# Half-precision passes for the second half of a filter's transform, placed behind the first projections' second token halves

## The reference

```
hy, q, k, v, nq, nk, nv = split(modulate(rms_norm(x)) @ w_in)   # hy: 768 columns
filt = hyena_filter(...)        # sine network, times a decay: forward and backward taps, 256 channels
u = short_conv(hy)              # 3 taps along the tokens, 768 channels: v, x1, x2
v = v * x1
y = irfft(rfft(v, 2S) * rfft(filt, 2S))[:S]
out = x2 * (y + v * skip)
```

## Time and profile before

| | us |
|---|---|
| median of three timed runs | 1261.15 (1258.84 to 1262.37) |
| the profiled execution | 1259.79 |
| its span, first to last instruction | 1258.0 |
| PE busy | 1228.7 (98%) |
| DVE busy | 975.1 (78%) |
| ACT busy | 657.3 (52%) |
| POOL busy | 402.0 (32%) |
| granted TensorE clock, mean | 0.999 of full |

### The profile page before, as it was taken

How to read it: one execution, slowest core, us unless ns; L and a number is a source line. 1 busy time by engine, 2 the same in 40 slices (tenths; PEclk the granted TensorE clock), 3 DMA queues, 4 the chain that set the end, 5 groups by cost and what they waited for, 6 DMA issues and landing times. The chain is left out here.

```text
span 1258.0 us, 23349 instructions
## 1 busy us (share of the span) xinstructions
PE 1228.7 (98%) x8052; PEld 667.3 (53%) x8052; DVE 975.1 (78%) x1583; ACT 657.3 (52%) x1244; POOL 402.0 (32%) x381
## 2 busy tenths in 40 slices
PE   8999999999999999999999999999999999999997
PEld 1564656556675666664454455455545554444443
DVE  3879998676778999964379888888888885666587
ACT  2632234556779999963135644555455553412425
POOL 0100000114678999850031244455544430000001
PEclk9999999999999999999999999999999999999999
DMA  9728723235200130021300332322233307997953
GB/s 355 276 75 327 253 83 134 68 90 154 65 31 2 34 134 5 29 85 51 117 34 2 101 91 87 96 73 74 83 98 100 100 25 260 350 335 248 357 205 134
DMA packets 111030, 164.16 MB, mean 130 GB/s; under 512 B 8560, under 2 KB 70000, under 8 KB 109552
## 3 DMA queue, kind: packets, MB, share of 16 engines
q1 hardware_dynamic: 110960, 163.24, 37.8%
HBM read 138.57 MB, written 22.55 MB: 128 GB/s over the span
## 5 line engine op out<-in xcount | busy, mean ns | idle before, releaser
L1307 PE MATMUL PS<-arena 128*128 128x512 f16 (+9 forms) x7452 | 1187.2, 320 | 18.0 <-DMA arena<-in_w_mod 5.4
L1307 PEld LDWEIGHTS PS<-arena 128*128 128x128 f16 (+3 forms) x7452 | 616.5, 100 | 562.7 <-issue 37.9
L3094 DVE SCALAR_TENSOR_TENSOR arena<-arena 128x512 f16<-128x512 f32 x128 | 113.2, 890 | 29.8 <-ACT arena L2342 29.3
L2342 ACT ACTIVATE arena<-arena 128x512 f16<-128x512 f32 x120 | 75.3, 630 | 98.5 <-PE PS L1307 98.5
L2470 ACT ACTIVATE arena<-arena 128x512 f16<-128x512 f32 x77 | 48.1, 629 | 126.2 <-DVE arena L3314 75.1
L2986 DVE TENSOR_REDUCE arena<-PS 128x1 f32<-128x512 f32 (+1 forms) x160 | 106.5, 680 | 9.1 <-PE PS L1307 9.1
L2241 ACT ACTIVATE arena<-PS 128x512 f16<-128x512 f32 x140 | 88.3, 631 | 1.2 <-PE PS L1307 0.7
L1301 POOL TENSOR_TENSOR arena<-arena 128x1 f32<-128x1 f32 x8 | 4.8, 606 | 232.1 <-DVE arena L3468 232.1
L1157 POOL TENSOR_TENSOR arena<-arena 128x512 f16<-128x512 f32 x64 | 74.0, 1159 | 9.4 <-ACT arena L2244 8.1
L3151 DVE TENSOR_TENSOR arena<-PS,arena 128x256 f32<-128x256 f32 (+1 forms) x100 | 55.1, 552 | 24.8 <-PE PS L1307 24.5
L3010 DVE TENSOR_TENSOR arena<-PS,arena 128x512 f16<-128x512 f32 x96 | 65.4, 682 | 4.0 <-ACT PS L2244 3.9
(11 more groups left out here) (220 smaller groups left out, 1287.3 us busy)
## 6 DMA issues: line engine op xcount, KB each, us to landing
arena<-in_w_ffn_out SPq DMA_DIRECT2D x121, 256.0 KB, 5.0
arena<-in_w_mod SPq DMA_DIRECT2D x23, 1024.0 KB, 7.3
arena<-in_w_ffn_in SPq DMA_DIRECT2D x88, 256.0 KB, 3.0
left_operands<-arena SPq DMA_DIRECT2D x43, 256.0 KB, 3.0
arena<-in_w_in SPq DMA_DIRECT2D x9, 1024.0 KB, 5.5
arena<-left_operands SPq DMA_DIRECT2D x3, 2816.0 KB, 13.0
arena<-lay_bias SPq DMA_DIRECT2D x12, 512.0 KB, 3.9
arena<-in_x SPq DMA_DIRECT2D x2, 2048.0 KB, 13.5
```

The costliest lines, as they stand in the source:

```text
L1307: return pe.matmul(out, lhsT, rhs, start=start, stop=stop, skip_group_check=True)
L2342: act.activation(block_split(p, b)[:, 0], weight_block(p, b), ACT.Copy, scale=WS).then_inc(blk_hi, 1)
L3094: dve.scalar_tensor_tensor(dst[:, 1], src, WS, dst[:, 0], ALU.mult, ALU.subtract).then_inc(blk_lo, 1)
```

## The change

The second half of the filter's transform (kt = 1) is done in three f16 passes instead of f32. Its table comes as high and low halves (fwd2, scaled by 2^10; the same 1 MB), and the taps are split into halves too (filt16, neg16, scaled by 2^8): four copies on ACT and four subtractions on DVE, made after the last tokens have been split. The first half of the transform (kt = 0) stays in f32. The 24 products become 72. They stand behind the second token halves of ct 0 and 1 now, where they stood ahead of them. On ACT and DVE the work that needs the spectrum moves behind the convolution of ct 1, with the half of chunk 11 behind that of ct 0. Late product 1 comes behind the spectrum, late 2 and 3 behind it.

```
+            def filter_sums_16():
+                c = chunk_index("ff", 1)
+                arrived(pe, c)
+                w = raw16(c, NT * 2, 2, P)
+                even, odd = (0, 1), (2, 3, 6, 7)
+                high = (4, 5)
...
+                    pe.wait_ge(filt_lo, 1 + ready + 1)
+                    for bank, cols, parts in groups:
+                        for i, (nt, trig, src) in enumerate(parts):
+                            for part, other in ((0, 0), (0, 1), (1, 0)):
+                                ins = mm(PS[:, bank, 256 * cols:256 * cols + 256], w[:, 2 * nt + trig, part], src[:, other],
+                                         i == 0 and part + other == 0, i == len(parts) - 1 and part == 1)
+                ins.then_inc(spec_mm, 1)
...
-            arrived(pe, chunk_index("ff", 1))
+            pe.wait_ge(hT_rdy, 16)
+            for ct in range(2):
+                pe.wait_ge(hT_f, 19 + ct)
+                hyena(ct, (1,))
             pe.wait_ge(spec_rdy, 1)
-            for part in range(6):
-                filter_sums(1, part)
-            pe.wait_ge(hT_rdy, 16)
-            pe.wait_ge(hT_f, 20)
-            for ct in range(2):
-                hyena(ct, (1,))
+            filter_sums_16()
...
-            even_filter(1)
-            hi_of(chunk_index("hy", 1), spl(1, KD, 256))
+            for n, (dst, src, scale) in enumerate((
+                    (filt16[:, 0, 0], filt_a, FS), (filt16[:, 0, 1], filt_b, FS),
+                    (neg16[:, 0, 0], filt_a[:, 6:8], -FS), (neg16[:, 0, 1], filt_b[:, 2:4], -FS))):
+                act.activation(flat(dst), flat(src), ACT.Copy, scale=scale).then_inc(even_part, 1)
...
+                if ct == 0:
+                    act.wait_ge(spec_mm, 1)
+                    hi_of(chunk_index("hy", 1), spl(1, KD, 256))
                 if ct == 1:
+                    even_filter(1)
                     hi_of(chunk_index("hy", 2), spl(0, KD, 256))
...
             late(0)
-            filter_spectrum(1)
-            lo_of(chunk_index("hy", 1), spl(1, KD, 256))
+            for n, (dst, hi, src, scale) in enumerate((
...
+                dve.wait_ge(even_part, 3 + n + 1)
+                dve.scalar_tensor_tensor(flat(dst), flat(src), scale, flat(hi), ALU.mult, ALU.subtract).then_inc(filt_lo, 1)
...
+                if ct == 0:
+                    lo_of(chunk_index("hy", 1), spl(1, KD, 256))
                 if ct == 1:
+                    filter_spectrum(1)
+                    late(1)
                     lo_of(chunk_index("hy", 2), spl(0, KD, 256))
-                for n in ((1, 2), (3,), (4, 5), (6, 7), (), ())[ct]:
+                for n in ((), (2, 3), (4, 5), (6, 7), (), ())[ct]:
```

More of the change, by code:

```diff
@@ L36 @@
 CV, CG = 2.0 ** -3, 2.0 ** 2
+FS = 2.0 ** 8
 MAGIC = 1.5 * 2.0 ** 23
@@ L489, in build @@
         neg_a, neg_b = f32(44, 2, HYW), f32(46, 2, HYW)
+        filt16 = f16(Z + 59, 2, 2, NT, HYW)
+        neg16 = f16(Z + 75, 2, 2, 2, HYW)
         xs = f32(Z + 59, 10, D)
@@ L675, in build @@
         left_in["A22"], left_in["S3"] = near_in[1], x_in[1]
+        filt_lo = mcol_mm
         part_hi, part_lo = taps_mm, taps_rdy
@@ L882, in load @@
                         sp.wait_ge(split_lo, n_split(before))
-                sp.dma_start((raw16 if CHUNKS[c] in ("fwd", "inv") else raw)(c, *shape), src).then_inc(raw_in[chunk_slot(c)], 16)
+                sp.dma_start((raw16 if CHUNKS[c] in ("fwd", "inv") or c == chunk_index("ff", 1) else raw)(c, *shape), src).then_inc(raw_in[chunk_slot(c)], 16)
             sp.dma_start(cols[:, 0:N_COLS], lay["cols"]).then_inc(cols_in, 16)
@@ L910, in _ @@
                     load(c, w_in[:, :, 256 * n:256 * n + 256], (8, 256))
+                elif kind == "ff" and n == 0:
+                    load(c, cst["fwd"][n].rearrange("p a b k -> p (a b) k"), (16, P))
                 elif kind == "ff":
-                    load(c, cst["fwd"][n].rearrange("p a b k -> p (a b) k"), (16, P))
+                    load(c, cst["fwd2"][n].rearrange("p a b c k -> p (a b c) k"), (32, P))
                 elif kind == "fwd":
@@ L1364, in filter_sums @@
                         .then_inc(spec_mm, 1)
+            def filter_sums_16():
[4 more added lines that the diff above has]
+                high = (4, 5)
+                for ready, groups in enumerate((
+                        [(4, 0, [(nt, 0, filt16[:, :, 0, nt]) for nt in even]),
+                         (5, 0, [(nt, 0, filt16[:, :, 0, nt]) for nt in high]),
+                         (6, 0, [(nt, 0, filt16[:, :, 0, nt]) for nt in odd])],
+                        [(4, 1, [(nt, 1, filt16[:, :, 1, nt]) for nt in even]),
+                         (5, 1, [(nt, 1, filt16[:, :, 1, nt]) for nt in high]),
+                         (6, 1, [(nt, 1, filt16[:, :, 1, nt]) for nt in odd])],
+                        [(7, 0, [(nt, 1, filt16[:, :, 0, nt] if nt < 4 else neg16[:, :, 0, nt - 6]) for nt in odd])],
+                        [(7, 1, [(nt, 0, neg16[:, :, 1, nt - 2] if nt < 4 else filt16[:, :, 1, nt]) for nt in odd])])):
+                    pe.wait_ge(filt_lo, 1 + ready + 1)
[5 more added lines that the diff above has]
+                ins.then_inc(spec_mm, 1)
             def forward(kt):
@@ L2666, in filter_spectrum @@
             def filter_spectrum(kt):
-                a = CG / (1024 * TS * CV)
+                a = CG / (1024 * TS * CV) / (TS * FS if kt else 1)
                 f = [flat(F[:, kt, j]) for j in range(4)]
-                dve.wait_ge(even_part, 2 + kt + 1)
+                dve.wait_ge(even_part, 2 + 5 * kt + 1)
                 own.step(dve.scalar_tensor_tensor(fp, PS[:, 5], a, f0, ALU.mult, ALU.add))
@@ L2718, in _ @@
             late(0)
-            filter_spectrum(1)
-            lo_of(chunk_index("hy", 1), spl(1, KD, 256))
+            for n, (dst, hi, src, scale) in enumerate((
+                    (filt16[:, 1, 0], filt16[:, 0, 0], filt_a, FS), (filt16[:, 1, 1], filt16[:, 0, 1], filt_b, FS),
+                    (neg16[:, 1, 0], neg16[:, 0, 0], filt_a[:, 6:8], -FS), (neg16[:, 1, 1], neg16[:, 0, 1], filt_b[:, 2:4], -FS))):
+                dve.wait_ge(even_part, 3 + n + 1)
+                dve.scalar_tensor_tensor(flat(dst), flat(src), scale, flat(hi), ALU.mult, ALU.subtract).then_inc(filt_lo, 1)
             for ct in range(6):
@@ L2766, in residue_sums @@
                 (a, b, c, d), bank = half_sums, lambda n: PS[:, n].rearrange("p (a k) -> p a k", a=2)
-                dve.wait_ge(even_part, 4 + 2 * kt + 1)
+                dve.wait_ge(even_part, 8 + 2 * kt + 1)
                 own.step(dve.tensor_tensor(a, r0, bank(5), ALU.add))
                 own.step(dve.tensor_tensor(b, r0, bank(5), ALU.subtract))
-                dve.wait_ge(even_part, 4 + 2 * kt + 2)
+                dve.wait_ge(even_part, 8 + 2 * kt + 2)
                 own.step(dve.tensor_tensor(c, r1, bank(7), ALU.add))
```

2 lines of the change are left out of this document (1 added, 1 removed).

## The result

| | before | after |
|---|---|---|
| median of 20 timed runs each, side by side, us | 1259.07 | 1263.12 |
| all runs, us | 1257.47 to 1263.59 | 1261.15 to 1267.93 |
| ratio to before, with its 95% interval | | 1.0027 [1.002, 1.0034] |
| span of the profiled execution, us | 1258.0 | 1262.6 |
| PE / DVE / ACT busy, us | 1228.7 / 975.1 / 657.3 | 1230.1 / 980.9 / 660.8 |

A forecast was written before the change was run, and what follows sets the result against it. PE was taken as the bound, DVE close behind: minus 2.65 us for the products plus 5.25 us of new waits gave +2.6 us, so 1263.1 us from the mean of four runs, 1260.54; range 1258 to 1266.3 us.

The forecast's parts named there:

- PE is the bound, DVE close behind.: From 60 to 300 us PE waited only 3.3 us; DVE's lateness by 122 us reaches PE at 174.40 us.
- The products: 7.86 instead of 10.5 us, and the transform's end at 97.05 us.: Second filter transform on PE: 72 half-precision products replace 24 full-precision ones, saving 2.65 us, running from 89.2 to 97.05 us.
- The splits: no PE wait.: ScalarE's copies done by 85.1 us, DVE's subtractions by 89.25 us, covered by 10.4 us of moved projections; no PE wait.
- The chain through DVE.: After the later-freed slot, DVE waits for late weights; third convolution starts at 115.6 us, 3.0 us late, 2.6 remaining.
- the data stream was continuous, so its landing shifts by the same 7.75 us: Late product 2's weight, queued behind the filter table's slot, lands at 110.45 us instead of 102.7 us.
- rival 2: Late weights 2 and 3 land together at 112.95 us, late product 2 starts 2.5 us later; sum +5.1 us, chance 0.15.
- PE's two meetings.: PE waits 3.6 us for late product 7 near 130 us, then meets DVE again at 174.40 us.
- At 174.40 us it is behind by all of DVE's 2.6 us.: At the transposes of the query, key and value part, PE is late by DVE's remaining delay, 2.6 us.
- A shift at 174.40 us stays to the end.: After 174.40 us PE waits only 2.1 us near 298 us, behind engines that follow PE, so the delay persists.
- Rival 1: PE's saving from the products comes through: minus 2.65 us, 1257.9 us; chance 0.12.
- Rival 3: Queued transfers drain faster and DVE waits little or not at all; sum -1.5 to -0.2 us, chance 0.12.
- Rival 4: PE waits for a split near 89 us because a ScalarE copy starts late; with 2 us, 1265 us; chance 0.03.

The follow-up runs named there:

- Run 2: Kernel before, with only SP's order edited: third projection weight and rope tables issued ahead of late weight 1; 1260.67 us, ratio 0.9995 to before.
- run 10: Changed kernel with third weight and rope tables issued first, rope scaling in DVE's wait near 198 us, late columns behind v's first transposes; 1257.29 us, 0.9970 of before.
- run 11: Kernel before with three rearrangements (SP issue order, rope scaling in DVE's wait, columns behind transposes), transform in full precision at its old place; 1261.12 us, 0.9997 of before.
- run 4: Kernel before with the splits' four copies and four subtractions added, results unread, transform still f32 in its old place; 1262.56 us, ratio 1.0006 to before.
- run 6: Half-precision transform with its splits at the old place and in the old order, without the two projections as cover; 1265.95 us, ratio 1.0041 to before.
- Run 3: Changed kernel with 15 unused products keeping PE busy ahead of the second late group's columns; 1263.15 us, ratio 1.0018 to before.
- run 1: Changed kernel with the third projection weight and rope tables issued on SP ahead of late weight 1; 1258.60 us, ratio 0.9982 to before.
- run 5: Changed kernel's order with the transform's second half still in f32 and no splits, the move alone; 1267.89 us, ratio 1.0055 to before.
- run 7: Changed kernel with only the two rope tables issued later, behind the load of late product 5; 1262.57 us, ratio 1.0013 to before.
- run 9: Changed kernel with third weight and rope tables issued first, and rope scaling moved into DVE's wait near 198 us; 1259.50 us, ratio 0.9983 to before.
- run 8: Changed kernel with third weight and rope tables issued first, and rope scaling on DVE moved to about 225 us; 1261.80 us, ratio 1.0000 to before.

## Why the prediction was right, and where it was not

**PE is the bound, DVE close behind.** Right. Run 2 shows it from the other side: in before, DVE's third convolution 1.5 us earlier only made DVE wait for PE at the next one.

**The products: 7.86 instead of 10.5 us, and the transform's end at 97.05 us.** Right: ACT's copy behind it starts at 97.05 us, forecast 97.15. What they are worth in time is less clear: by run 10 against run 11, 3.8 us of medians, but 1.4 to 1.9 us at T.

**The splits: no PE wait.** Right, by the trace and by run 4; without the cover 6.66 us, by run 6. ACT took 4.74 us for the four copies and DVE 5.69 for the four subtractions, where I had 5.0 and 5.94.

**The chain through DVE.** The waits came where they were said to be: 1.74, 0.97, 2.20, 0.89 and 1.08 us, against 1.2, 0.8, 2.3, 1.0 and "just in time". The landings were forecast at 102.3, 105.3, 110.45 and 112.95 and came at 102.4, 105.4, 110.5 and 114.3. The last one is a miss of 1.35 us: of "the data stream was continuous, so its landing shifts by the same 7.75 us" only three of four held. The window from 110.5 to 114.3 us moved 1.54 MB, at 405 GB/s; late weight 3 is 1.05 MB of that at most. The rest, 0.49 MB at least, is of weights issued later: of late weight 4, issued at 105.17 us, 5.3 us behind it, and perhaps of the next, issued at 109.7 us. By the Trainium skill (DMA: Bandwidth & Descriptors, Queues, rings and completion order) descriptors of a ring are taken in ring order but completions need not follow it; the trace goes no further than that: the weights landed in the order of their issue, but a later one moved data before an earlier one had landed. I had weighed it for weights 2 and 3 (rival 2), not for a weight issued much later. With it the third convolution was 4.3 us late, not 3.0.

**PE's two meetings.** The wait for the late columns came at 3.36 us plus 1.46 us before the projection in front of them, 4.8 instead of 3.6. The forecast didn't name the meeting at that projection; with the third convolution at the forecast 115.6 us it would have come to some 0.1 us. The transposes of v started 3.0 us later than before. Here the forecast had PE 1 us behind; most of the difference is that 1.35 us landing and about 0.5 us of columns at the lower clock (above).

**The step that failed: "At 174.40 us it is behind by all of DVE's 2.6 us."** It was behind by 5.7. Between the transposes of v and T stand 2.75 us (0.76 + 1.99) in which PE did the same work at half the clock. The forecast had no term for that; a wait of 3.6 us stood in it at full price and no more. With the DVE chain alone, 4.3 less the regained 0.5 us, T would have come 3.8 us late; the clock made PE later than DVE, and DVE waited for PE's transposes instead (1.8 us in all between 123 and 200 us). Run 3 shows the term: with PE kept busy T is 2.0 to 2.1 us earlier, counted from the same start, and PE waits for DVE again.

**"A shift at 174.40 us stays to the end."** Not all of it. Up to the attention's last such transposes it does: from T to them PE takes 108.6 us before and 108.7 with the change. Then the wait of 2.1 us near 298 us is 0.56 here, with another of 0.25 behind it, and span less T is 1.1 us shorter (1082.5 against 1083.6). At T the late landing adds 1.2 us to the forecast of 2.6 and the clock another 1.9 beyond DVE's 3.8: 5.7 us, less the 1.1 given back is the span's 4.6. The timed runs put the change at 3.4 to 4.05. So a landing that was put too early and a clock that wasn't counted, with some given back, stand behind a time that came out as forecast.

**The rivals.** Rival 1 (the saving comes through) needs DVE not to be late; with SP's order changed it nearly is so, in run 1, and in run 10. Rival 2 (the two weights land together) fails by the trace: 110.5 and 114.3 us, 3.8 us apart. Rival 3 fails: the fourth megabyte landed 13.5 us after the first was issued (97.0 to 110.5), as before, and not 10. Rival 4 fails, as said. Two side sums of the forecast are slightly off, with no bearing on it: 4 MiB in about 10 us from 97.1 us land near 107.1 us, not 107.6, and 1.1 us sooner with 0.5 regained is -1.6 us, not -1.5.

**What stays open.** PE's wait near 300 us was 0.5 to 4.35 us long in the thirteen traces: 2.1 in before, 0.56 with the change, 4.35 in run 4, 1.9 in run 10. It doesn't follow T, and in some traces the clock falls behind it, as here in run 4:

```profile
300.12 2.05 PE L1311 MATMUL PS<-arena 128*128 128x384 f16 x21 [4.35 <-DVE arena L2978]
```

```profile
295.00:300.00 5.00, 0.78 (x4) 0.16 (x2) 0.49 (x2) 1.33 (x4) 1.25 (x1) 0.91 0.31 17
300.00:305.00 5.00, 4.88 (x31) 3.33 (x32) 2.31 (x8) 2.88 (x8) 1.16 (x1) 0.50 0.97 356
```

PE, DVE and ACT all stand nearly still there while little data moves (17 GB/s). No run was made to find its cause, and one trace of each kernel can't tell how often it is short. The length alone doesn't decide whether the clock falls: it fell after 1.99 us in run 5, and not after 2.07 us in before and in run 7. It is a likely part of the several us by which executions of one kernel differ: of the 79 timed runs of before beside the experiments, the 19 with a mean granted clock of 0.999 took 1260.2 us on average, the 6 with 0.996 took 1263.5 us. Where in these runs the clock fell isn't recorded. So the 1.1 us given back are read from one trace of each kernel, and whether the change or chance did it isn't shown; nor is it shown why the medians of runs 5, 9, 10 and 11 differ by other amounts than their T.

## What to carry to other kernels

Moving work that frees a buffer moves everything that stands behind that buffer's next load in the issuing queue, needed or not: before such a move, look which of the queued transfers need the slot at all, and issue the others first. A saving on the bounding engine is kept only if the engine next to it, here DVE, is early by as much at the next place where they meet. And price a new wait on PE with what may follow it: in this kernel 3.4 us of waiting cost PE another 2.75 us (and some 0.5 more in the columns) at the lower clock, of which some 2 us arrived at the attention.

## What the runs showed of the hardware

- The granted clock fell to 0.50 after PE waits of 3.36 us (the change), 3.35 (run 5), 2.89 (run 7) and 6.66 (run 6), but also after one of 0.45 us (run 8); it did not after 0.58 (run 1), 0.71 (run 9), 1.36 (run 3) and 1.46 us (the change, before its fifth projection). The length of one wait alone does not decide it. In the change, and in runs 5, 7 and 8, the work right behind the wait was sixteen products of one column; but runs 1 and 9 had these too, without a fall.
- Transfers of 1 MB that were issued 5.3 us and more behind another on the same queue took part of the data rate before the first had landed (1.54 MB moved in the last 3.8 us before it did): that one took 14.4 us to landing and came 3.8 us behind its forerunner, where 1 MB at the 405 GB/s of that window is 2.6 us.
- Three f16 passes of 256 columns took 3 x 0.109 us against 0.435 us for one f32 product of the same shape, three quarters of the time.
